# GpSimd adds the three squared tiles of a scan group, and the group's sum of squares moves behind the second weight tile

## What is computed

```python
def ssd_output(y, xs, z, d_skip, norm_g):
    b, l = y.shape[:2]
    y = (y + d_skip[..., None] * xs).reshape(b, l, SSD_INNER) * jax.nn.silu(z.astype(jnp.float32))
    yg = y.reshape(b, l, SSD_GROUPS, SSD_INNER // SSD_GROUPS)
    yg = yg * lax.rsqrt(jnp.mean(yg * yg, axis=-1, keepdims=True) + NORM_EPS)
    return (yg.reshape(b, l, SSD_INNER) * norm_g.astype(jnp.float32)).astype(z.dtype)
```

## Time and profile before

| | |
|---|---|
| median of 3 runs | 1256.17 us (1255.94 to 1259.31) |
| profiled execution | 1255.79 us, span 1253.7 us |
| PE busy | 1209.5 us (96%) |
| DVE busy | 826.5 us (66%) |
| ACT busy | 567.3 us (45%) |
| POOL busy | 85.1 us (7%) |
| products of `ysum` (L1914) | 24 half products, from 217.7 to 430.3 us |
| chain of waits, whole span | PE 75%, DVE 14%, ACT 5%, issue 4%, DMA 2% |

### The profile page before, as it was taken

The page is one execution under the profiler, slowest core; times in us unless marked ns, Lnnn a source line. Parts: engine busy times, 40 slices in busy tenths (PEclk is TensorE's granted clock), DMA queues, the critical chain, the costliest instruction groups (busy, mean ns, idle before and its releaser), DMA issues.

```text
span 1253.7 us, 17502 instructions
## 1 busy us (share of the span) xinstructions
PE 1209.5 (96%) x6580; PEld 961.9 (77%) x6580; DVE 826.5 (66%) x1205; ACT 567.3 (45%) x981; POOL 85.1 (7%) x73
## 2 busy tenths in 40 slices
PE   5999899999998999999999999999999899999998
PEld 3567688787877787787887887886787569888997
DVE  3663587896977563786585684785765894655655
ACT  3541363746556422731331331423744674744543
POOL 0000101001020015000000000034000004000000
PEclk9999999999999999999999999999999999999999
DMA  9667011111111224253553543541233003455554
GB/s 350 249 263 265 21 56 67 57 58 51 61 58 34 80 90 171 104 198 124 187 176 135 199 151 134 201 151 67 85 136 120 31 2 135 138 187 194 185 186 151
DMA packets 41838, 166.37 MB, mean 133 GB/s; under 512 B 4528, under 2 KB 6704, under 8 KB 38704
## 3 DMA queue, kind: packets, MB, share of 16 engines
q1 hardware_dynamic: 41488, 164.97, 37.4%
q10 hardware_dynamic: 288, 0.56, 0.1%
HBM read 164.46 MB, written 1.05 MB: 132 GB/s over the span
## 4 chain that ended last, share of the span: by engine, by line
PE 75%; DVE 14%; ACT 5%; issue 4%; DMA 2%; DVEq 0%; SPq 0%; ACTq 0%
PE ps L1677 49%; PE ps L1684 8%; PE ps L1942 7%; DVE cacc L1378 3%; PE ps L1767 1%; PE ps L1700 1%; DVE sm L1625 1%; ACT ey L1091 1%; ACT u L987 1%; DVE ey L1452 1%; DVE prob L1650 1%; DVE mixF L1478 1%; PE ps L2039 1%; PE ps L1840 1%; DVE w_lo L1228 1%
## 5 line engine op out<-in xcount | busy, mean ns | idle before, releaser
L935 ACT ACTIVATE w_hi<-raw 128x1024 fp32r<-128x1024 f32 x206 | 216.6, 1053 | 234.6 <-DMA raw<-in_w_ff 178.5
L1228 DVE TENSOR_TENSOR w_lo<-raw,w_hi 128x1024 fp32r<-128x1024 f32 x206 | 256.3, 1244 | 97.6 <-ACT w_hi L935 97.3
L1677 PE MATMUL ps<-a_hi,w_hi 128*128 128x512 f32 (+1 forms) x868 | 318.5, 367 | 0.4 <-DVE w_lo L1228 0.4
L1677 PE MATMUL ps<-a_hi,w_lo 128*128 128x512 f32 (+1 forms) x868 | 307.6, 354 | 0.0
L1677 PE MATMUL ps<-a_lo,w_hi 128*128 128x512 f32 (+1 forms) x868 | 307.4, 354 | 0.0
L1677 PEld LDWEIGHTS ps<-a_hi,w_hi 128*128 128x128 f32 x868 | 164.1, 189 | 28.3 <-issue 3.4
L1677 PEld LDWEIGHTS ps<-a_lo,w_hi 128*128 128x128 f32 x868 | 164.2, 189 | 25.0 <-issue 1.0
L1677 PEld LDWEIGHTS ps<-a_hi,w_lo 128*128 128x128 f32 x868 | 164.0, 189 | 23.2
L1677 PE MATMUL ps<-b_hi,w_hi 128*128 128x512 f32 x304 | 119.2, 392 | 0.0
L1677 PE MATMUL ps<-b_lo,w_hi 128*128 128x512 f32 x304 | 118.4, 390 | 0.0
L1677 PE MATMUL ps<-b_hi,w_lo 128*128 128x512 f32 x304 | 118.3, 389 | 0.0
(11 more groups left out here) (256 smaller groups left out, 1700.9 us busy)
## 6 DMA issues: line engine op xcount, KB each, us to landing
raw<-in_w_ff SPq DMA_DIRECT2D x128, 512.0 KB, 3.4
mring<-in_w_mod SPq DMA_DIRECT2D x24, 1024.0 KB, 6.9
mring<-in_w_mod SPq DMA_DIRECT2D x32, 768.0 KB, 5.2
raw<-in_w_in_even SPq DMA_DIRECT2D x36, 512.0 KB, 3.5
raw<-in_w_in_odd SPq DMA_DIRECT2D x18, 512.0 KB, 3.5
raw<-in_w_out_even SPq DMA_DIRECT2D x16, 512.0 KB, 3.5
raw<-in_w_out_odd SPq DMA_DIRECT2D x8, 512.0 KB, 3.4
bias<-in_rpb_na SPq DMA_DIRECT2D x8, 256.0 KB, 3.8
```

The lines of the kernel that those rows point to most:

```text
L935: nc.scalar.activation(w_hi[:, u % RING, :, :], raw[:, u % RING, :, :], ACT.Copy).then_inc(hi_done, 1)
L1228: v.tensor_tensor(w_lo[:, u % RING, :, :], raw[:, u % RING, :, :], w_hi[:, u % RING, :, :].bitcast(F32), ALU.subtract).then_inc(lo_done, 1)
L1677: ins = mm(out_ap, w_[:, n % RING, k, :], (x_[k][:, 0:ntok] if type(x_) is list else x_[:, k, 0:ntok]), start=(k == 0 and j == 0), stop=(k ...
```

## The change

Groups are counted from 0, and `ysum` of group `g` stands in the steps of group `g + 1`, or behind the last group for group 3. For groups 0, 1 and 3, GpSimd adds the second and the third squared tile to the first, one addition after the other, and TensorE multiplies only the first tile by the matrix of ones. For groups 0 and 1 the step `ysum` stands behind slot 1 instead of behind slot 0, and `ynorm` behind slot 2 instead of behind slot 1. For group 2 all is as it was, since the third `z` tile of group 3 overwrites `gate` early. Behind the last group `ysum` stands after `outA` 4 instead of after `outA` 3, and `ynorm` after the `mixsplit` steps 2 and 3 of the second half instead of before them. A new semaphore `ysum_done` counts GpSimd's additions. The lines left out give it its name.

```diff
--- before.py
+++ after.py
@@ -227,15 +227,17 @@
             s.append(("cb", g))
         s.append(("seg", g, "f", ch[0]))
         slot(0)
-        if g:
+        if g == G - 1:
             s.append(("ysum", g - 1))
         states(0, 3)
         s.append(("seg", g, "b", ch[0]))
         states(3, 3)
         mixsplits(0, 0)
         slot(1)
-        if g:
+        if g == G - 1:
             s.append(("ynorm", g - 1))
+        elif g:
+            s.append(("ysum", g - 1))
         mixsplits(0, 1)
         for n in range(NCH):
             if n < NCH - 1:
@@ -245,6 +247,8 @@
                 s.append(("yt", g, ch[n - 1]))
             s.append(("yoff", g, ch[n]))
             slot(2 + n)
+            if n == 0 and 0 < g < G - 1:
+                s.append(("ynorm", g - 1))
             if n < NCH - 1:
                 s.append(("seg", g, "b", ch[n + 1]))
             mixsplits(0, *((), (5,), (), ())[n])
@@ -259,12 +263,12 @@
             s += [("toks", g + 1, c_) for c_ in ch[2:]]
         s.append(("ygate", g))
     gemm("outA", 3)
+    gemm("outA", 4)
     s.append(("ysum", G - 1))
-    gemm("outA", 4)
     mixsplits(1, 0, 1)
     gemm("outA", 5)
+    mixsplits(1, 2, 3)
     s.append(("ynorm", G - 1))
-    mixsplits(1, 2, 3)
     gemm("outA", 6)
     mixsplits(1, 4, 5)
     gemm("outA", 7)
...
@@ -891,7 +895,7 @@
             pool.wait_ge(consts_set, 4)
             for i in range(2):
                 pool.memset(one32[:, i, i:i + 1], 1.0).then_inc(consts_set, 1)
-            n_acc = n_tmp = 0
+            n_acc = n_tmp = n_add = 0
             for st in steps:
                 if st[0] == "norm" and st != NORM0:
 
@@ -910,6 +914,14 @@
                         else:
                             pool.tensor_tensor(acc, hs, hs, ALU.mult).then_inc(acc_sq, 1)
                         n_acc += 1
+                elif st[0] == "ysum" and st[1] != G - 2:
+                    g = st[1]
+                    pool.wait_ge(ysq_done, g + 1)
+                    for i in range(1, XT):
+                        n_add += 1
+                        if i > 1:
+                            pool.wait_ge(ysum_done, n_add - 1)
+                        pool.tensor_tensor(gate[:, 0, :], gate[:, 0, :], gate[:, i, :], ALU.add).then_inc(ysum_done, 1)
                 elif st[0] == "state":
 
                     _, g, d, ch = st
@@ -1906,12 +1918,16 @@
                         ins = mm(ps[:, b, P * i:P * i + P], ycomb[:, n % 2, P * i:P * i + P], ident, start=False, stop=True, skip_group_check=True)
                     ins.then_inc(filling(st), 1)
                 elif k == "ysum":
-                    pe.wait_ge(ysq_done, st[1] + 1)
+                    tiles_ = XT if st[1] == G - 2 else 1
+                    if tiles_ == 1:
+                        pe.wait_ge(ysum_done, (XT - 1) * (st[1] + 1 - (st[1] == G - 1)))
+                    else:
+                        pe.wait_ge(ysq_done, st[1] + 1)
                     b = jobs[st][0]
                     if free_before[st]:
                         pe.wait_ge(*emptied(st))
-                    for i in range(XT):
-                        ins = mm(ps[:, b, :], ones, gate[:, i, :], start=(i == 0), stop=(i == XT - 1))
+                    for i in range(tiles_):
+                        ins = mm(ps[:, b, :], ones, gate[:, i, :], start=(i == 0), stop=(i == tiles_ - 1))
                     ins.then_inc(filling(st), 1)
                 elif k == "grow":
                     pe.wait_ge(modc_done, MG0 + MG1)
```

More of the change, by code:

```diff
@@ L635, in trunk @@
         mod1_in = [sem(f"mod1_in{i}") for i in range(MR1)]
-        names = ("grow_done htok_done unit_done sines_done hv_done mfull_done dtrow_done acc_sq tmp_sq mu_used row_done mcol_done modc_done sil_done hi_done lo_done c0_in dft_in xsq_done xrms_done xr_done xn_done xnt_done xu_done c1_in vec_in wdt_in bias_in dve_seq act_seq consts_set vt_done "
+        names = ("ysum_done grow_done htok_done unit_done sines_done hv_done mfull_done dtrow_done acc_sq tmp_sq mu_used row_done mcol_done modc_done sil_done hi_done lo_done c0_in dft_in xsq_done xrms_done xr_done xn_done xnt_done xu_done c1_in vec_in wdt_in bias_in dve_seq act_seq consts_set vt_done "
                  "silc_done th0_done h_done sq_done var_done rstd_done nt_done u_done split_done coef_done "
@@ L645, in trunk @@
         S = {n: sem(n) for n in names}
-        (grow_done, htok_done, unit_done, sines_done, hv_done, mfull_done, dtrow_done, acc_sq, tmp_sq, mu_used, row_done, mcol_done, modc_done, sil_done, hi_done, lo_done, c0_in, dft_in, xsq_done, xrms_done, xr_done, xn_done, xnt_done, xu_done, c1_in, vec_in, wdt_in, bias_in, dve_seq, act_seq,
+        (ysum_done, grow_done, htok_done, unit_done, sines_done, hv_done, mfull_done, dtrow_done, acc_sq, tmp_sq, mu_used, row_done, mcol_done, modc_done, sil_done, hi_done, lo_done, c0_in, dft_in, xsq_done, xrms_done, xr_done, xn_done, xnt_done, xu_done, c1_in, vec_in, wdt_in, bias_in, dve_seq, act_seq,
          consts_set, vt_done, silc_done, th0_done, h_done, sq_done, var_done, rstd_done, nt_done,
```

## The result

| | before | after |
|---|---|---|
| median of 14 runs each, same chip | 1256.65 us (1254.61 to 1259.31) | 1261.24 us (1258.62 to 1264.21) |
| profiled execution, its span | 1255.79 us, 1253.7 us | 1264.21 us, 1262.1 us |
| PE busy | 1209.5 us | 1208.9 us |
| POOL busy | 85.1 us | 96.1 us |
| products of the sums | 24 half products | 12 half products |

What follows compares the result with a forecast made beforehand. ScalarE's and VectorE's queues were taken to set the end of the middle groups, not TensorE's products. Two groups at 0.85 + 1.4 us, less 1.7 in the tail, gave +2.8 us: 1259.0 us, range 1255.0 to 1262.0.

Steps and rivals of the forecast that it cites:

- The tail: Behind the last group: TensorE runs without a wait there, so two products fewer save 1.7 us.
- Rival C: Whole kernel: TensorE is the bound and every product taken away counts, 5.2 us saved, 1251.0 us; chance 0.12.
- The order and the collisions: Each middle group: later logarithm and moved normalisation, 0.85 us, plus GpSimd holding up VectorE, 1.4 us.
- The logarithm and the normalisation: Middle groups: logarithm behind slot 1, normalisation behind the second convolution; VectorE gets the next decay later, +0.85 us a group.
- the state multiplications: Middle groups: GpSimd's last two, started earlier, run into VectorE's operation at 219.83, about +0.46 us.
- the update that no longer meets GpSimd: Middle groups: VectorE's update after the copies meets nothing, where it lost 0.1 us before.
- The additions: Middle groups: GpSimd's first holds VectorE's low weights about 1.0 us; the second waits for them and runs beside copies.
- Rival B: Middle groups: hardly any collision of GpSimd with VectorE, 0 to 0.9 us a group, 1256.2 to 1258 us; chance 0.20.
- The hole's size: TensorE's wait in front of the fourth state product: 2.3 us without collision, 3.7 with.
- D: Middle groups: TensorE's clock falls behind the hole, 24 products pay about 2.1 us in each of two groups, 1263; chance 0.13.
- E: Tail gives nothing because ScalarE's later logarithm holds up weights or splits, 1260.7 us; chance 0.10.

Runs made afterwards that it cites:

- with the hole filled: Changed kernel plus three unused products in front of the fourth state product of both middle groups: 1258.24 us, ratio 1.0023 to the kernel before.
- the run without the additions: Changed kernel with GpSimd's additions left out, only the first squared tile entering the sums of groups 0, 1 and 3: 1259.9 us, ratio 1.0037 to the kernel before.

## Where the prediction was right, and where it was short

**Direction, place and sign: right.** The tail gives 1.69 us (forecast 1.7), the products saved don't make the middle groups shorter, and these groups get longer by the order and by GpSimd's collisions. Rival C, a stage that pays for every product, is out: after has two products fewer a group and is longer, and three products instead of one in the new place cost 0.6 us, not 1.7.

**The order and the collisions: right in sum, 2.25 forecast, 2.1 to 2.2 measured with the hole filled.** By terms:

- The logarithm and the normalisation (0.85) with the state multiplications (0.46) and the update that no longer meets GpSimd (-0.1): 1.21 forecast, 1.04 measured without the additions. The decay product is 1.33 us, +0.37 and not +0.46. It is 1.32 us without the additions too (218.16), so it is GpSimd's state multiplications that hold it. The order's own share of the 1.04 was not measured by itself.
- The additions: 1.0 forecast, 1.09 measured. The second waited for the low weights, as forecast, but the first had waited too: it was asked for while the decay product was running. The two take 1.98 and 2.14 us in the record, where the first of the two behind the last group takes 1.30 us.

The Trainium skill, "SBUF — State Buffer", section "Who interferes with whom", had it that a VectorE instruction with two SBUF inputs and a GpSimd instruction that reads SBUF lock each other out, and that a VectorE instruction with at most one SBUF input, outside the modes that use both ports, doesn't contend. The trace agrees: the low weights take 2.28 us beside an addition and 1.21 without, and the two copies out of PSUM, with the second addition beside them, take 1.21 us in both. Rival B is out.

**The clock: put down as a rival with 0.13, and it took part.** The step that fell short is the sum, which has the clock behind the hole at nothing. The hole's size was right, 3.7 us forecast with the collision, 3.54 and 3.48 measured. But the rows at hand had only a gap of 1.79 us without slow products and one of 10 us with them, so I left the clock to chance. The prices by the stretches are 0.7 us in the second group and 1.4 in the third (76.61 and 77.16 less the 75.88 and 75.76 of the filled hole), by the medians 2.2 us for both (4.6 less 2.4). My price for D was 2.1 us a group, 24 products of slot 1 at +0.087 us each. Both factors were off: in the third group the slow products of slot 1 stand 0.43 us apart (305.34 and 305.77) in place of 0.23, so +0.20 each, but no more than the first three of them are at that speed, and in the second group none. The rest of the price lies on the state products. So the forecast's mechanism stood, and the missing 2 us are a term that I had in a rival and should have had in the sum at half the size.

That the time lies inside the range is partly luck. It is outside the band that the forecast had by itself (1258.2 to 1260.0); the range went on to 1262.0 for E and for a D in one group alone, and what came was both groups at about half of D's price.

The Trainium skill, "TensorE: Matmul & The Clock Gate", section "Why this matters for your kernels", warned of idle gaps between bursts of products. The trace agrees in direction (clock 0.53 behind the hole). It doesn't settle which hole is long enough: behind 2.41 us the clock stayed in the kernel with the new order and three products and fell in the one without the additions.

**The signs named ahead.** Single product of 0.86 us: seen. Slot 1 of the second group at about 226.4: it was 227.07 on before's time scale, 0.7 us later by the slow state products. Low weights +1.0: +1.06. A stall of about 4 us before VectorE's decay product: 4.60. A wait of over 1 us at the last SiLU in place of 0.47: 1.07 us. Middle groups near 75.9: 75.8 without the clock, 76.6 and 77.2 with it. First products of slot 1 at twice their spacing, the sign of D: in the third group only, for its first three (304.34 to 306.20). This line shows the wait at the last SiLU:

```profile
281.06 0.55 PE L1862 MATMUL ps<-c,xbc 128*128 128x128 f32 x3 [1.07 <-DVE xbc L1403]
```

What stays open: why the clock differs from one execution to the next. Among the 14 executions of after the mean clock goes from 0.994 to 0.999, and the two shortest (1258.62 and 1258.66 us) have 0.998 and 0.999. These two lie at the forecast without the clock. Whether the fall is missing there at these very holes isn't shown, since one execution alone has a trace.

## What to carry to other kernels

A stage in which TensorE is busy 98% of the time can still be ordered by another engine's queue: look at who ends the last wait before each burst, and put work into the place where TensorE waits before you take work away from it. Work given to an idle GpSimd can be paid by VectorE, here 1.09 us a group: look for a VectorE instruction with two SBUF inputs that stands beside it, and for what hangs on that one. A saved product that leaves a hole can cost more than the product, since the clock behind the hole may be the lower one: price the hole as well as the product.

## What the runs showed of the hardware

- Holes of TensorE and the products behind them, all in the same place of the kernel: 0.7 to 1.0 us (filled holes) and 1.59 us left them at full speed; 2.41 us once left them and once not; 2.47 us, twice, and 3.48 and 3.54 us slowed them. A pair of half products takes 1.62 us instead of 0.88 then. The first pairs behind a hole can still run at full speed (the first behind 2.47 us in the run without the additions, the first two behind 3.48). A fall cost 0.7 to 1.4 us of the group's time. That holes this short sufficed I had not expected.
- GpSimd and VectorE took turns in the order of asking here: the first addition was held by VectorE's decay product, then held VectorE's low weights for 1.06 us, and the second was held by these. The waiting shows as longer records: the two additions stand at 1.98 and 2.14 us, where the first one behind the last group takes 1.30.
- ScalarE's table load (1.28 us) runs while the instruction that needs it still waits for its input: in the kernel with three products behind slot 1 it lies at 232.68, and the logarithm starts at 234.57, 0.6 us after the load's end.
